# Convolved FFNs that take their norm at eviction: the inverse root moves from the input to each unit's output

## The reference

```python
def rms_norm_2(x, g):
    xf = x.astype(jnp.float32)
    y = xf * lax.rsqrt(jnp.mean(xf * xf, axis=-1, keepdims=True) + NORM_EPS)
    return (y * g.astype(jnp.float32)).astype(x.dtype)

def conv_ffn(h, w_up, conv_w, conv_b, w_down):
    u = causal_dwconv(h @ w_up, conv_w, conv_b)
    gate, up = jnp.split(u, 2, axis=-1)
    return (jax.nn.silu(gate) * up) @ w_down

for i in range(DEPTH):
    ...
    x = x + rms_norm_2(h, post_g)
    h = conv_ffn(rms_norm_2(x, ffn_pre_g[i]), ffn_w_up[i], ffn_conv_w[i], ffn_conv_b[i], ffn_w_down[i])
    x = x + rms_norm_2(h, ffn_post_g[i])
```

## Time and profile before

| | us |
|---|---|
| median of 3 runs | 1729.79 (1725.6 to 1733.93) |
| the profiled execution | 1728.21 |
| its span | 1726.4 |
| TensorE busy | 1659.5 (96%) |
| VectorE busy | 1225.8 (71%) |
| ScalarE busy | 952.5 (55%) |

### The profile page before, as it was taken

One profiled execution on the slowest core, in us unless ns is written; L12 is line 12 of the kernel. 1 busy time (PEld: TensorE's weight loads), 2 busy tenths in 40 slices (PEclk: granted clock), 3 DMA queues, 4 the chain that ended last, 5 costly groups with the idle time before them and its releaser, 6 DMA issues.

```text
span 1726.4 us, 29017 instructions
## 1 busy us (share of the span) xinstructions
PE 1659.5 (96%) x10776; PEld 1483.9 (86%) x10776; DVE 1225.8 (71%) x2006; ACT 952.5 (55%) x1638; POOL 7.1 (0%) x16
## 2 busy tenths in 40 slices
PE   7999999999999999998999999989999999899997
PEld 6888897898888888886888889868999888789986
DVE  6677666677777777676677766667787666577875
ACT  6555554565555555557565554455665444456653
POOL 1000000000000000000000000000000000000000
PEclk9999999999999999999999999999999999999999
DMA  7554563255546554551355456314544653235452
GB/s 285 193 176 152 191 221 125 90 203 194 185 149 212 193 192 152 193 184 56 105 197 193 165 170 248 110 40 182 194 173 148 215 220 111 86 122 193 157 168 91
DMA packets 47505, 286.32 MB, mean 166 GB/s; under 512 B 5885, under 2 KB 6653, under 8 KB 24369
## 3 DMA queue, kind: packets, MB, share of 16 engines
q1 hardware_dynamic: 45216, 278.94, 45.9%
q10 hardware_dynamic: 1808, 5.39, 0.8%
q0 software_dynamic: 384, 0.68, 0.1%
HBM read 283.94 MB, written 1.05 MB: 165 GB/s over the span
## 4 chain that ended last, share of the span: by engine, by line
PE 88%; DVE 6%; ACT 4%; issue 1%; DMA 0%; ACTq 0%; SPq 0%; DVEq 0%
PE ps_gemm L175 34%; PE ps_gemm L182 31%; PE ps_gemm L183 16%; DVE s_wlo L90 2%; ACT s_whi L81 1%; PE ps_s L911 1%; PE ps_gemm L942 1%; ACT s_work L964 1%; PE ps_sum L223 1%; PE ps_gemm L911 0%; DMA s_wraw<-in_stream_dram 0%; PE ps_gemm L932 0%; PE ps_sum L863 0%; PE ps_t L932 0%; DVE s_xn L316 0%
## 5 line engine op out<-in xcount | busy, mean ns | idle before, releaser
L90 DVE TENSOR_TENSOR s_wlo<-s_wraw,s_whi 128x1024 fp32r<-128x1024 f32 (+3 forms) x602 | 623.1, 1077 | 376.3 <-ACT s_whi L81 376.3
L81 ACT ACTIVATE s_whi<-s_wraw 128x1024 fp32r<-128x1024 f32 (+3 forms) x600 | 531.7, 934 | 393.6 <-PE ps_gemm L183 202.9
L182 PE MATMUL ps_gemm<-s_xr,s_whi 128*128 128x512 f32 x1408 | 492.5, 396 | 1.0 <-DVE s_work L637 1.0
L183 PE MATMUL ps_gemm<-s_xr,s_wlo 128*128 128x256 f32 x1408 | 391.6, 278 | 0.0
L175 PE MATMUL ps_gemm<-s_xr,s_whi 128*128 128x256 f32 x2128 | 387.8, 285 | 3.4 <-DVE s_xr L326 1.7
L182 PE MATMUL ps_gemm<-hid_r,s_whi 128*128 128x512 f32 x1056 | 370.8, 394 | 2.9 <-DVE hid_r L600 2.9
L175 PEld LDWEIGHTS ps_gemm<-s_xr,s_whi 128*128 128x128 f32 x2128 | 332.2, 192 | 8.6 <-issue 6.1
L182 PEld LDWEIGHTS ps_gemm<-s_xr,s_whi 128*128 128x128 f32 x1408 | 264.2, 188 | 64.6 <-issue 2.2
L175 PE MATMUL ps_gemm<-s_xr,s_wlo 128*128 128x256 f32 x1064 | 301.0, 283 | 0.0
L183 PE MATMUL ps_gemm<-hid_r,s_wlo 128*128 128x256 f32 x1056 | 294.7, 279 | 0.0
L183 PEld LDWEIGHTS ps_gemm<-s_xr,s_wlo 128*128 128x128 f32 x1408 | 264.8, 188 | 0.1
(11 more groups left out here) (381 smaller groups left out, 1500.9 us busy)
## 6 DMA issues: line engine op xcount, KB each, us to landing
s_wraw<-in_stream_dram SPq DMA_DIRECT2D x177, 1024.0 KB, 4.8
s_wraw<-in_stream_dram SPq DMA_DIRECT2D x96, 704.0 KB, 4.1
s_wraw<-in_stream_dram SPq DMA_DIRECT2D x16, 768.0 KB, 4.3
s_wraw<-in_stream_dram SPq DMA_DIRECT2D x16, 512.0 KB, 3.4
s_room<-in_o_bias_dram ACTq DMA_DIRECT2D x1, 3072.0 KB, 11.9
s_room<-in_mem_dram SPq DMA_DIRECT2D x4, 256.0 KB, 6.0
s_x<-in_x_dram SPq DMA_DIRECT2D x1, 1024.0 KB, 12.3
s_room<-in_e_alibi_dram ACTq DMA_DIRECT2D x1, 1024.0 KB, 5.9
```

The source lines that it names most:

```text
L81: c.act.activation(c.whi[:, slot, s], c.wraw[:, raw, s], ACT.Copy).then_inc(c.hi_ready, 1)
L90: last = c.dve.tensor_tensor(c.wlo[:, slot, s], c.wraw[:, raw, s], c.whi[:, slot, s].bitcast(F32), ALU.subtract)
L182: pe.matmul(bank, w_hi, x_both, start=k == 0, stop=False)
L183: return pe.matmul(left, w_lo, x_hi, start=False, stop=k == ks - 1)
```

## The change

`mix_e` and `mix_o` are followed by the kind "late" instead of "norm", and `conv_0` and `conv_1` join `LATE_SCALED`. So both FFNs take the residual times the norm weight as input. In each iteration VectorE multiplies the whole unit (gate and value, 128x512) by the inverse root out of the PSUM bank into a new SBUF tile `cv_raw` and frees the bank. ScalarE's and VectorE's taps read `cv_raw`. ScalarE therefore waits for `bank_free` ahead of its taps, and the end of VectorE's taps has a semaphore of its own, `value_ready`.

```diff
-AFTER = {"mix_e": "norm", "conv_0": "late", "mix_o": "norm", "conv_1": "out"}
-LATE_SCALED = ("ffn1_0", "mix_a", "ffn2_0", "ffn1_1", "mix_b", "ffn2_1", "mix_e", "mix_o")
+AFTER = {"mix_e": "late", "conv_0": "late", "mix_o": "late", "conv_1": "out"}
+LATE_SCALED = ("ffn1_0", "mix_a", "ffn2_0", "ffn1_1", "mix_b", "ffn2_1", "mix_e", "mix_o", "conv_0", "conv_1")
...
         if j == 0:
-            last = first_products_pe(c, cnt, banks, u, (c.xlo_ready, cnt.xn + 1), late)
+            last = first_products_pe(c, cnt, banks, u, (c.xlo_ready, cnt.xn + 1), late,
+                                     None if wide else POST_GROUPS["late"])
...
         else:
+            act.wait_ge(c.bank_free, g0 + j + 1 + step)
             for side in range(2):
-                act.activation(c.cv[:, j % 2, side, :], c.ps_gemm[:, (g0 + j) % 4, side * T:(side + 1) * T], ACT.Identity,
+                act.activation(c.cv[:, j % 2, side, :], c.cv_raw[:, j % 2, side, :], ACT.Identity,
...
         split_lo(c, u0 + j + 2, None if turn is None else (turn, 4))
+        bank = c.ps_gemm[:, (g0 + j) % 4, :].rearrange("p (s t) -> p s t", t=T)
+        dve.wait_ge(c.unit_done, u0 + j + 1 + step)
+        dve.tensor_tensor(c.cv_raw[:, j % 2, :, :], bank, c.inv[:, :].unsqueeze(1).to_broadcast([P, 2, T]),
+                          ALU.mult).then_inc(c.bank_free, 1)
         if j:
             gate(j - 1, step)
-        bank = c.ps_gemm[:, (g0 + j) % 4, :]
         dve.wait_ge(c.tap_ready, 2 * m + 2 + step * 2)
...
-                ins = dve.scalar_tensor_tensor(v, bank[:, side * T:(side + 1) * T - back],
+                ins = dve.scalar_tensor_tensor(v, c.cv_raw[:, j % 2, side, 0:T - back],
                                                tap(c, conv, j, side, 2 - back, turn), v, ALU.mult, ALU.add)
-                ins.then_inc(c.back_done if back == 1 else c.conv_ready if side == 0 else c.bank_free, 1)
+                ins.then_inc(c.back_done if back == 1 else c.conv_ready if side == 0 else c.value_ready, 1)
         if j:
             rest(j - 1, turn)
-        dve.wait_ge(c.bank_free, g0 + j + 1 + step)
+        dve.wait_ge(c.value_ready, m + 1 + step)
...
+        c.cv_raw = c.room[:, 0:4 * T].rearrange("p (j s t) -> p j s t", j=2, t=T)
```

More of the change, by code:

```diff
@@ L558, in ffn_act @@
     cnt.conv += conv is not None
-    cnt.late += late
+    cnt.late += late and conv is None
     u0, g0 = u0 + NF, g0 + (NF if conv is not None else 2 * NF)
@@ L2824, in build @@
         c.conv_ready = sem("conv_ready")
+        c.value_ready = sem("value_ready")
         c.scaled_ready = sem("scaled_ready")
@@ L2943, in _ @@
                 load_stage(c, name, dict(STAGE_UNITS)[name])
-            stored = sum(len(POST_GROUPS[kind]) for kind in ("norm", "late", "norm"))
+            stored = sum(len(POST_GROUPS[kind]) for kind in ("late", "late", "late"))
             for g, (first, n) in enumerate(POST_GROUPS["out"]):
```

## The result

The kernel got slower, and by more than forecast. The changed kernel takes 1758.16 us (median of 4 runs, 1755.99 to 1760.15), the kernel before 1729.14 in the same comparison: a ratio of 1.0162, 95% interval 1.0142 to 1.0181. Forecast were 1746 and at most 1755. The profiled execution took 1757.44 us, with a span of 1755.6.

The account below looks back on a forecast made before the run. TensorE, busy 96%, bounds the kernel before; then VectorE's chain with ScalarE would bound the up loops. Two conv stages lose 21.8 us, less 5.2 at the transitions: 16.6 more, 1744.8, plus 1.6 for the median: 1746, range 1734 to 1755.

Parts of the forecast that it names:

- some 15 us: Conv stages' up loops: TensorE's waits for the split weights (L90) grow from nothing to this, 0.4 a unit.
- the rival in which they get cheap and the chain fits: VectorE's four taps save 0.5 us reading SBUF, period 5.7, TensorE stays the bound: 1727 on the median; chance 0.13.
- The entries' gain: From L316 to the second unit behind both mixers: 12.84 us instead of 15.45 and 15.47, 5.2 us saved in all.
- the rival in which they give nothing: Something in a mixer's end holds the first products back, no transition gain: 1751; chance 0.09 together with the clock.
- the drain: Beside ScalarE's table load, about 1380 ns by the skill; taken as absent, otherwise 2.8 us more.
- the chain step: VectorE's period per up unit, waits for ScalarE included: 5.98 us outside the loop, 6.20 inside, against TensorE's 5.77.
- ScalarE hears of it: 0.03 outside: Handover from the end of VectorE's new multiplication to ScalarE's taps: 0.03 us outside the loop, 0.14 inside.
- The first iteration: VectorE's iteration 0 of the up units, without gate or rest, was put at 5.76 us.
- The tail's own waits: First down tile: TensorE waits 1.1 us for the second half's weights, 3.1 instead of 0.5 for the last hidden tile.
- the clock as a rival: TensorE's tail waits lower its clock, 2.8 us a tail, 1752 if in both; chance 0.09 together with lost transitions.
- 10.9 forecast: Loss of each conv stage: last up unit 7.2 us late plus 3.7 in the tail.
- upper bound of 6.26: VectorE's period per unit with 0.15 us at each crossing and ScalarE's taps at 1.10.

Follow-up runs that it names:

- experiment 3: New entries alone: kind late behind both mixers, loop of the kernel before, units left unscaled: 1725.47 us, ratio 0.9977 to the kernel before.
- Experiment 4: Changed kernel with the loop of units 4 to 19 written out on VectorE and ScalarE in the convolved FFNs: 1749.13 us, ratio 1.0109.
- experiment 5: Changed kernel with the new multiplication split into two of 128x256, so ScalarE may start after the first: 1743.79 us, ratio 1.0077.
- experiments 6 to 8: Changed kernel with useless TensorE products in the tail's waits, five and nine: 1757.20 us; two and four: 1753.47; changed kernel itself again: 1755.84.
- the second comparison: The unaltered changed kernel measured once more, beside its version with fillers: 1755.84 us, where the kernel before took 1731.88, ratio 1.0139.
- experiment 2: New loop alone: post norms as in the kernel before, units scaled by the inverse root a second time: 1752.52 us, ratio 1.0137.
- experiment 1: Changed kernel with VectorE's multiplication ahead of the two subtractions instead of behind them: 1723.24 us against 1728.16 before, ratio 0.9966.

## Why the prediction was wrong in size and right in kind

**Right.** That VectorE's step would grow past TensorE's; that the wait for ScalarE's taps would do it (1.06 a unit, "about 1 us"); that TensorE would wait for the split weights in the up loops and for hid_r in the first down tile; that nothing else in these stages would be late. The sign it named, "some 15 us" of such waits, reads 11.4 in the trace although both stages start their last up unit 10.2 us late (125.4 behind the second unit's mark, before 115.3). The trace's idle time understates the wait, at least in part because the records of the matmuls ahead reach into it (0.28 long, one every 0.12): a step of 6.29 is 0.53 above 5.76, and its wait is noted as 0.30 (at 1260.05). The taps on VectorE kept their price in SBUF: 479 ns, so the rival in which they get cheap and the chain fits is out, and the rule of the Trainium skill (VectorE: DVE Perf Modes, section Mode 2x_2P) agrees with that. The entries' gain is 4.5 in the first profile and would be 5.2 at the clock of the second one (12.83 and 12.85), as forecast; the rival in which they give nothing is out by experiment 3. From the logarithm to the next rounding it is 2.24 us (1198.08 to 1200.32), the number taken from the earlier trace rows; the drain that the Trainium skill names beside a table load (ScalarE: Activation LUTs, section What ACT_TABLE_LOAD costs) is not there, as the prediction had it.

**Wrong: the items of the chain step.** The sum said 5.98 outside and 6.20 inside.
- "ScalarE hears of it: 0.03 outside". It was 0.81 from the multiplication's start to ScalarE's, so 0.13 behind its 0.683. The row it came from the earlier trace rows was a handover into another operation; why this one takes longer, no run shows. Outside, the other items come to 0.04 more together, and the step is 6.12.
- Inside, the multiplication to ScalarE 0.85 (forecast 0.82), ScalarE to VectorE 1.27 (1.20; 1.24 in the unit behind it), the four taps 1.58 (1.56): 6.29 to 6.33.
- The first iteration was put at 5.76. The sum's own items without rest give 5.98 - 0.34 = 5.64, and the working has no source for the 0.12 between; it measured 5.91.
- The turn of the loop isn't in the sum at all. It adds 0.27 to one step in four. TensorE never showed it, because it waited for nobody there.

By iteration 19 VectorE is at 123.0 behind the second unit's start in place of 120.07: 0.07 from the start (3.44 for 3.37), 0.15 and 0.42 from outside the loop, 1.5 from fifteen steps of 0.1 and 0.8 from three turns. The steps of iterations 19 and 20 add 0.24 (6.29 and 5.46 for 6.20 and 5.31). By the last hidden tile it is 3.2: TensorE goes on at 143.2 (1341.24 - 1198.04), forecast 140.0. The tail's own waits were close: 1.18 (forecast 1.1) and 0.42 + 2.23 = 2.65 (3.1). Experiment 4 gives the loop's whole part, 3.65; experiment 5 shows that an item's price goes through to the time: 0.27 less a step is 5.8 us by the last hidden tile and 5.6 in conv_1, where both kernels lost the clock.

**Wrong: the clock as a rival.** The prediction priced it at 2.8 a tail and against it held that the waits are short "with work between them". It happened, at half that: 1.4 in each tail (experiments 6 to 8). So it belonged into the forecast with part of its price, not outside it.

Together, for one stage: 10.9 forecast + 3.2 chain + 1.45 clock = 15.6, as measured. For both that is 9.3, the first entry's clock adds 0.7: 16.6 + 10.0 = 26.6 of the 26.8. How the working came to its upper end of 1755 it doesn't say. Its upper bound of 6.26 for the step adds 1 to 2 us a stage and reaches 1748 to 1750; the clock rival alone reached 1752. The same working with 6.12, 6.30 and the turns ends at 1752 to 1753, and with the clock at 1756, just outside. Measured were 1758 and, in the second comparison, 1756, where before was 2.7 slower too.

## What to carry to other kernels

When a step is put between two others on a busy engine, look first at who waits for its result, and put it where that wait has other work beside it: the same multiplication cost 31 us less over the two FFNs, one position earlier. Where two engines hand a unit back and forth, sum the relay from start to start, with the handovers and the turn of a loop in it, and take the loop's price as part of the forecast once TensorE is no longer the bound. And ask what TensorE's new wait does to its clock just behind it.

## What the runs showed of the hardware

**The clock after a short wait is not the same each time.** In experiment 5 the two convolved FFNs have the same waits, 2.24 and 2.23 us. Behind the first the next pairs follow at the full rate, 0.35 us apart, and the window around it (1328 to 1336) is granted 1.00; behind the second the clock falls:

```profile
1331.38 0.50 PE L182 MATMUL ps_gemm<-hid_r,s_whi 128*128 128x512 f32 x1 [2.24 <-DVE hid_r L604]
...
1328.00:1336.00 8.00, 5.61 (x31) 4.41 (x30) 5.41 (x11) 2.78 (x7) 0.00 (x0) 1.00 0.32 107
...
1673.89 0.51 PE L182 MATMUL ps_gemm<-hid_r,s_whi 128*128 128x512 f32 x1 [2.23 <-DVE hid_r L604]
...
1674.96 0.63 PE L182 MATMUL ps_gemm<-hid_r,s_whi 128*128 128x512 f32 x1
1675.61 0.63 PE L182 MATMUL ps_gemm<-hid_r,s_whi 128*128 128x512 f32 x1
```

This makes most of the 1.85 us between its 195.07 and 196.92; 0.3 more is there before, mostly from one step of 6.25 in conv_1's loop. In experiment 2 only the second of the two tails lost it, which is its 198.92 against 200.50. In the two profiles of after, three of the four tails lost 1.3 to 1.5 us and one 2.7.

**The wide FFNs run at two speeds.** They aren't touched by the change. From one table load to the next (about one FFN), the second and the fourth wide FFN of after:

```profile
379.54 1.28 ACT L512 ACT_TABLE_LOAD   x1
...
521.74 1.28 ACT L366 ACT_TABLE_LOAD   x1
...
878.75 1.28 ACT L512 ACT_TABLE_LOAD   x1
...
1023.05 1.28 ACT L366 ACT_TABLE_LOAD   x1
```

142.2 us and 144.3 us, at a granted clock of 1.00 in both, with TensorE waiting for nothing in the hundred microseconds from 400 and from 900. TensorE's step for a unit is 5.545 or 5.65 us. In before, one of the four took 144.3, in experiment 1 all four, in after two, in its second profile three; over all eleven profiles 32 of 44. So it comes by execution, in steps of 2.1 us, and a difference of 2 to 6 us between two single profiles can be this alone. It is why I compare stages by their marks. What sets it, no run here shows.

**What a loop costs on VectorE and ScalarE:** 0.17 us a unit for addresses and waits that a register holds, and 0.27 more for each turn, seen only where these engines are the chain.
